# Token pairs for the compression product stored by their place modulo eight

## The reference

```python
n_cmp = (S - CMP_LEN) // CMP_STRIDE + 1
tok_idx = jnp.arange(n_cmp)[:, None] * CMP_STRIDE + jnp.arange(CMP_LEN)[None, :]

def compress(t, pe, w1, w2):
    blocks = t[:, :, tok_idx] + pe
    flat = blocks.reshape(B, G, n_cmp, CMP_LEN * DK)
    return jax.nn.silu(flat @ w1) @ w2
```

## Time and profile before

| what | value |
|---|---|
| three runs | 1454.55, 1455.14, 1455.33 us |
| median | 1455.14 us |
| profiled execution | 1455.89 us, its span 1453.7 us |
| TensorE busy | 1419.3 us, 98% of the span |
| VectorE, ScalarE, GpSimd busy | 871.0, 622.7, 161.5 us |
| line 1942 on TensorE | 64 matmuls, two for each product |

### The profile page before, as it was taken

How to read it: one execution, slowest core, us unless ns; L and a number is a source line. 1 busy time by engine, 2 the same in 40 slices (tenths; PEclk the granted TensorE clock), 3 DMA queues, 4 the chain that set the end, 5 groups by cost and what they waited for, 6 DMA issues and landing times.

```text
span 1453.7 us, 21619 instructions
## 1 busy us (share of the span) xinstructions
PE 1419.3 (98%) x7942; PEld 1215.5 (84%) x7950; DVE 871.0 (60%) x1630; ACT 622.7 (43%) x1235; POOL 161.5 (11%) x178
## 2 busy tenths in 40 slices
PE   7999999999999999998999999999999999999999
PEld 6888888887888888897988878888888788888887
DVE  3002682106766776669793596655566598579764
ACT  5013303216555545460440477655555554444441
POOL 2433333521000000000242000000000000000000
PEclk9999999999999999999999999999999999999999
DMA  5211114200000000012111015444445956643332
GB/s 178 59 51 51 44 36 131 73 0 8 1 2 1 1 1 2 1 45 116 30 51 36 30 65 182 150 149 141 155 158 169 333 174 214 203 127 94 101 110 87
DMA packets 78253, 129.41 MB, mean 89 GB/s; under 512 B 8973, under 2 KB 26826, under 8 KB 78154
## 3 DMA queue, kind: packets, MB, share of 16 engines
q1 hardware_dynamic: 77968, 128.01, 27.6%
q10 hardware_dynamic: 186, 0.08, 0.0%
HBM read 94.51 MB, written 33.55 MB: 88 GB/s over the span
## 4 chain that ended last, share of the span: by engine, by line
PE 89%; DVE 7%; issue 2%; ACT 2%; DMA 1%; SPq 0%; DVEq 0%; ACTq 0%
PE ps L518 66%; PE ps L2105 6%; PE ps L2065 4%; PE ps L2080 4%; PE ps L2125 3%; PE ps L2049 1%; PE ps L1942 1%; PE ps L2099 1%; DVE hgrn_vg L1636 1%; PE ps L760 1%; DVE negmax L1495 1%; DMA x_in<-in_x_dram 1%; PE ps L2070 1%; PE ps L627 1%; DVE q_stack L1488 1%
## 5 line engine op out<-in xcount | busy, mean ns | idle before, releaser
L518 PE MATMUL ps<-mlp_w_low,hidden_high 128*128 128x512 f32 x448 | 174.4, 389 | 0.0
L518 PE MATMUL ps<-mlp_w_high,hidden_high 128*128 128x512 f32 x448 | 174.4, 389 | 0.0
L518 PE MATMUL ps<-mlp_w_high,hidden_low 128*128 128x512 f32 x448 | 174.4, 389 | 0.0
L518 PE MATMUL ps<-w_high,hT_high 128*128 128x512 f32 (+1 forms) x448 | 170.6, 381 | 0.8 <-ACT cmp_v L1072 0.7
L518 PE MATMUL ps<-w_high,hT_low 128*128 128x512 f32 (+1 forms) x448 | 168.3, 376 | 0.0
L518 PE MATMUL ps<-w_low,hT_high 128*128 128x512 f32 (+1 forms) x448 | 168.1, 375 | 0.0
L2105 PE MATMUL ps<-nsa,probs_T 128*128 128x64 f32 x1056 | 137.8, 274 | 0.0
L1298 ACT ACTIVATE mlp_w_high<-mlp_w_raw 128x512 fp32r<-128x512 f32 x112 | 70.6, 630 | 147.7 <-PE ps L518 147.7
L1667 DVE TENSOR_TENSOR mlp_w_low<-mlp_w_raw,mlp_w_high 128x512 fp32r<-128x512 f32 x112 | 76.9, 691 | 93.4 <-ACT mlp_w_high L1199 93.4
L2105 PEld LDWEIGHTS ps<-nsa,probs_T 128*128 128x128 f32 x1056 | 129.1, 193 | 0.0
L1747 DVE TENSOR_TENSOR mlp_w_low<-mlp_w_raw,mlp_w_high 128x512 fp32r<-128x512 f32 x112 | 77.2, 689 | 65.6 <-ACT mlp_w_high L1298 65.5
(11 more groups left out here) (233 smaller groups left out, 2846.3 us busy)
## 6 DMA issues: line engine op xcount, KB each, us to landing
hidden_raw<-hidden_pieces SPq DMA_DIRECT2D x112, 256.0 KB, 2.7
mlp_w_raw<-in_w_mlp_in_dram SPq DMA_DIRECT2D x32, 512.0 KB, 4.3
hidden_pieces<-hidden SPq DMA_DIRECT2D x64, 256.0 KB, 2.8
mlp_w_raw<-in_w_mlp_out_dram SPq DMA_DIRECT2D x64, 256.0 KB, 4.2
w_raw<-in_w_in_dram SPq DMA_DIRECT2D x56, 256.0 KB, 2.7
hidden_pieces<-hidden_s SPq DMA_DIRECT2D x48, 256.0 KB, 2.2
x_in<-in_x_dram SPq DMA_DIRECT2D x8, 512.0 KB, 7.6
w_raw<-in_w_out_dram SPq DMA_DIRECT2D x16, 256.0 KB, 2.8
```

The source lines that it names most:

```text
L518: ins = nc.tensor.matmul(out_ap, a_hl[i], b_hl[j], start=first and n == 0, stop=last and n == 2, skip_group_check=onto_a_sum_already_read)
```

## The change

`pairs` gets a dimension of eight: pair number i is stored under its remainder i mod 8, then by head, then by i div 8. One remainder holds 66 numbers for each of two heads, 132 side by side. Step n takes remainder n mod 8 and starts at n div 8; it streams 131 numbers in one run across both heads, where it took 130 with a step of eight. A head has 66 columns in the bank instead of 65; the column between the heads' parts that is read by nobody mixes both heads. The copies out of PSUM write eight runs of 32 numbers, and read for each run every sixteenth number of the bank, where they read every second. The copy of the position rows is split by heads, since the pattern has one dimension more. `w1`, the number of products and all waits stay.

```diff
--- before.py
+++ after.py
@@ -292,7 +292,8 @@
 
     w1 = sb("cmp_w1", [P, 2, CMP_STEPS, P], F32, HV_AT)
 
-    pairs = sb("cmp_tokens", [P, 2, NG, S // 2 + CMP_STEPS], F32, HV_AT + 16384)
+    CW = (S // 2 + CMP_STEPS) // 8
+    pairs = sb("cmp_tokens", [P, 2, 8, NG, CW], F32, HV_AT + 16384)
 
     KS_H = sb("k_high", [P, 2, NG, S], F32R, 0)
     KS_L = sb("k_low", [P, 2, NG, S], F32R, 16384)
@@ -594,8 +595,6 @@
 
     hid2 = nsa[:, 0, KC0:KC0 + 2 * P]
     hid_e = nsa[:, 1, KC0:KC0 + P].rearrange("p (g n) -> p g n", g=NG)[:, :, 0:NCMP]
-    CW = NCMP + 2
-
     hid_all = [ps[:, 4 + kv, 0:NG * CW].rearrange("p (g n) -> p g n", g=NG) for kv in range(2)]
     hid_ps = [h[:, :, 0:NCMP] for h in hid_all]
 
@@ -604,8 +603,8 @@
 
         for g in range(NG):
             for a in range(2):
-                eng_copy(pairs[a * DK:(a + 1) * DK, kv, g, b * BW // 2:(b + 1) * BW // 2],
-                         ps[g * DK:(g + 1) * DK, 4 + 2 * kv + b, a:BW:2]).then_inc(tok_pairs[b], 1)
+                eng_copy(pairs[a * DK:(a + 1) * DK, kv, :, g, b * BW // 16:(b + 1) * BW // 16],
+                         ps[g * DK:(g + 1) * DK, 4 + 2 * kv + b, a:BW:2].rearrange("p (q r) -> p r q", r=8)).then_inc(tok_pairs[b], 1)
 
 
     it = Items()
@@ -1049,8 +1048,10 @@
                     act.activation(f_, f_, func).then_inc(fm_done, 1)
 
             act.wait_ge(smallT, 1)
-            pe_rows = ps[:, 7, 0:2 * CMP_STEPS].rearrange("p (k s) -> p k s", k=2).unsqueeze(2).to_broadcast([P, 2, NG, CMP_STEPS])
-            act.activation(pairs[:, :, :, S // 2:], pe_rows, ACT.Copy).then_inc(smallT_out, 1)
+            pe_rows = ps[:, 7, 0:2 * CMP_STEPS].rearrange("p (k q r) -> p k r q", k=2, r=8)
+            for g in range(NG):
+                ins = act.activation(pairs[:, :, :, g, S // 16:], pe_rows, ACT.Copy)
+            ins.then_inc(smallT_out, 1)
             act.activation(lb[:, 0:2, :].rearrange("p a h -> p (a h)"), ps[:, 7, 64:64 + 2 * HH], ACT.Copy).then_inc(smallT_out, 1)
             act.wait_ge(hid_step, 3)
             act.activation(lb[:, 2:4, :], lb[:, 2:4, :], ACT.Exp).then_inc(lb_exp, 1)
@@ -1059,7 +1060,7 @@
                 pair_tokens(lambda o, i: act.activation(o, i, ACT.Copy), kv, 0)
             for kv in range(2):
                 act.wait_ge(hid_full, kv + 1)
-                act.activation(cbias[:, kv:kv + 1], hid_all[kv][:, 0, CW - 1:CW], ACT.Copy).then_inc(cb_ready, 1)
+                act.activation(cbias[:, kv:kv + 1], ps[:, 4 + kv, NCMP + 1:NCMP + 2], ACT.Copy).then_inc(cb_ready, 1)
                 act.wait_ge(cb_ready, kv + 1)
                 if kv:
                     act.wait_ge(hid_ready, 1)
@@ -1939,7 +1940,8 @@
                 for b in range(2):
                     pe.wait_ge(tok_pairs[b], 4 * (kv + 1))
                 for n in range(CMP_STEPS):
-                    ins = nc.tensor.matmul(hid_all[kv], w1[:, kv, n, :], pairs[:, kv, :, n:n + 8 * (CW - 1) + 1:8],
+                    ins = nc.tensor.matmul(ps[:, 4 + kv, 0:NG * CW - 1], w1[:, kv, n, :],
+                                           pairs[:, kv, n % 8, :, :].rearrange("p g n -> p (g n)")[:, n // 8:n // 8 + NG * CW - 1],
                                            start=n == 0, stop=n == CMP_STEPS - 1)
                 ins.then_inc(hid_full, 1)
```

## The result

The changed kernel takes 1446.13 us (median of six runs, 1445.44 to 1448.39), the kernel before in the same comparison 1455.08 us (six runs, 1454.39 to 1456.29). The ratio is 0.9943 with a 95% interval of 0.9932 to 0.9953. The medians differ by 8.95 us, 1.2 us more than the forecast.

What follows compares the result with a forecast made beforehand. TensorE was taken as the bound, busy 98% of the span. The median of 1455.14 us less 7.7 us of streaming, with copies, position rows and bias priced 0, gave 1447.4 us; range 1445.1 to 1449.8.

Steps and rivals of the forecast that it cites:

- The term of 7.7 us: Line 1942 on TensorE: 64 pieces fall from 0.236 to 0.115 us each, saving 7.7 us.
- Both ways to scale line 2125: Price of a new piece from line 2125: 0.1137 us if the weight load sets the pace, 0.1164 if the stream does.
- The copies: Sixteen copies of pairs out of PSUM on ScalarE and VectorE, hidden by TensorE's weight products; priced 0.
- upper bound of a doubling: Pair copies reading PSUM 64 bytes apart take at most twice as long, 0.76 and 0.84 us each.
- The break-even of 2.9 us a copy: Pair copies on VectorE: from 2.9 us each, seven times the present 0.42, the kernel is slower overall.
- The position rows: Their copy on ScalarE becomes two instructions, signal at most 0.22 us later, covered; priced 0.
- The release of weights: It moves earlier with the products; GpSimd's wait of 8.34 us before its cast shrinks to 4.5.
- The clock's room: TensorE's clock falls after a 2.04 us stand at 861.23 us; 1.6 us of room either way.
- the stride was not the cause: Rival, 0.08: float32 products of this stage are slow by themselves, pieces stay at 0.236 us; 1455.2 us.
- Half the gain: Rival, 0.04: runs must start on a line, so 32 of 64 pieces keep their price; 3.9 us saved, 1451.3.
- The copies can become the wait: Rival, 0.02: slow PSUM reads in 64-byte steps make TensorE wait; at 3.3 us a copy, 1458.4 us.
- given back later: Rival, 0.02: a wait behind 262 us with its own due time eats the gain, wholly (1455) or past it.

Runs made afterwards that it cites:

- step 3: Kernel before, old layout, keys' product reading every third number (12 bytes apart), values' every fourth; 5.57 us for the keys' set, 1453.49 us whole.
- step 4: Kernel before, old layout, values' product reading every fourth number (16 bytes apart), keys' every third; 7.39 us for the values' set, 1453.49 us whole.
- the groups of four: Kernel before, old layout, keys' product streaming 32 groups of 4 neighbours, 64 bytes apart, values' groups of 2; 1446.12 us inside lines, 1452.19 across borders.
- the layout alone: Changed kernel with its new layout and all copies, but the product walking in steps of 8, one segment of 130 columns; ratio to before 1.0006.
- four times 32 cut copies: Changed kernel with each copy of pairs cut into 32, 128 copies a set on either engine; median 1455.12 us, ratio to before 1.000.
- the two-segment kernel: Changed kernel with each product streaming two segments of 65 columns, one per head, instead of one of 131; median 1446.85 us, ratio to before 0.9942.
- steps 1 and 2 in the old layout: Kernel before, keys' product reading neighbouring pairs, values' every second pair; sets of 3.57 and 3.76 us, 1447.8 us whole.
- Step 16: Kernel before, 130 columns read as one segment, values' product in steps of 16 numbers, keys' in steps of 8; values' set 7.08 us, 1453.18 us whole.

## Why the prediction was right

*The path.* TensorE's chain was the bound, and each microsecond taken off it arrived. 7.96 us of the two sets are 7.95 us at the copy of `cmp_v`. In the recurrent mixer the long stretch of line 2125, which ended at 680.78 + 25.46 = 706.24 us, ends at 669.13 + 29.26 = 698.39 us in the chain of after, 7.85 us earlier.

*The cause.* It is the way the columns lie in memory, as the forecast had it from the earlier trace rows. The sharper form is from the runs: not the step of eight, but one line of 16 bytes for each column. The Trainium skill, "SBUF — State Buffer", section "Door 1: The DMA port swizzle", has the line of 16 bytes and the need for two hits in it, and the runs agree on both: two numbers in a line are nearly free, 3.68 and 3.76 us. The sentence behind it there names four float32 as the stride that is free; the runs differ from that, with 5.57 us for step 3 and 7.39 us for step 4, and the measurement decides.

*The price of a piece.* I took 0.115 us, between 0.111 and 0.118; it is 3.57/32 = 0.1116, at the lower bound. The term of 7.7 us was therefore 0.3 us too small. Both ways to scale line 2125 were too high: the 64 columns of line 2105, 0.111 us, were the nearer row. Why line 2125 takes 0.1137 us a piece for 128 columns, where the groups of four with as many columns take 0.1116, was not tried.

The Trainium skill's 81 ns for a matmul of 128 columns in a stream of loads and matmuls ("TensorE: Matmul & The Clock Gate", section "Back-to-back issue gap") is not what float32 pieces do here; they have 0.110 us even with 64 columns.

*The copies.* Priced 0 and measured 0: 380 and 423 ns against 379 and 422, and the layout alone ran at 1.0006. The upper bound of a doubling was needless; reading PSUM 64 bytes apart cost ScalarE and VectorE no more than 8 bytes apart. Their cover was tried both ways. The break-even of 2.9 us a copy is close: four times 32 cut copies made 10.3 us a set, 2.57 us for each former copy, and the time was level. By the forecast's rule 2.57 us a copy should have left 2.7 us of the gain. What I had left out is that the clock can fall behind such a wait, 1.9 us in this trace, which brings the point down.

*The position rows.* The copy to `lb` starts 0.17 us after the first copy instead of 0.12, and VectorE waits 1.16 us instead of 1.22: 0.05 us later, covered.

*The release of weights.* The wait of GpSimd was to shrink to 4.5 us and is 4.35. TensorE leaves the block at 254.58; 254.7 was said.

*The clock's room.* I gave 1.6 us either way to the fall of the clock behind the stand of 2 us. In this pair of traces it is 1.42 us. The 7.95 us of the sets and 1.42 us of this, less the 0.10 us by which the sets began later, make 9.3 us; the spans differ by 9.2. The runs of the changed kernel lie 3 us apart (1445.44 to 1448.39), three of them with a mean granted clock of 1.000, and these are the three shortest, 1445.44 to 1445.73. What sets in which execution the clock falls was not tried. The clock is not all of it: the profiled run of the two-segment kernel took 1447.93 us with a mean granted clock of 1.000, but its TensorE reached line 1971 at 49.58 us, where it was 48.33 in the trace after, and its first set 1.20 us later too (239.12 against 237.92). So the first 50 us, which the change does not touch, move the time too: that line starts between 47.21 and 49.58 us in the traces of these kernels.

*The measured difference.* No term of the sum gives 8.95 us; the change is worth the 7.95. The rest is most likely luck of the draw: four of the six runs lie at 1445.44 to 1446.53 us and two at 1448.3 and 1448.39, so the median is one of the lower group. Two other kernels with the same two sets of 3.57 us, four runs each, had medians 8.10 us (two segments) and 7.15 us (copies cut into eight) below the kernel before. All 14 runs of the three have the median 1447.04 us, close to the 1447.4 of the forecast.

*The rivals.* That the stride was not the cause fell with steps 1 and 2 in the old layout. Half the gain for a start off the line fell with the trace after, in which all pieces are alike. The copies can become the wait, but level with the gain only at some six times their length (2.57 against 0.42 us). Nothing was given back later.

## What to carry to other kernels

Look in the profile for float32 matmuls of equal shape and different duration; 416 against 275 ns was the whole find. The moving operand is paid by the lines of 16 bytes that it touches, so for pieces of this size a layout in which at least two neighbours of each line are read together is nearly enough (3.68 and 3.76 us a set), and full lines give the rest (3.57 us), whether in one run or in two. The engine that copies the operand into place did the reordering here for nothing (380 and 423 ns a copy, as before); its copies have to end before TensorE wants them.

## What the runs showed that I had not expected

A float32 product of 128 rows costs two pieces of 0.110 us, whether it streams 64 or 128 columns (3.52 and 3.57 us for 32 pieces); 192 columns take 0.85 ns a column, and a line costs 1.78 ns. Lines and floor don't add, the larger counts (step 3: 98 lines, 0.174 us); that the columns join in the same way rests on the one length above the floor. Step 16 is 6% faster than step 8 (7.08 against 7.57 us), and this stays open. And a wait of TensorE of 5.3 us in a stage at full clock cost 1.9 us more behind it.
